# Hybrid attention and mLSTM block: the split halves of gate weights and mLSTM values put side by side, two products in place of three

## The reference

```
qk = silu(causal_depthwise_conv(concat(mq, mk)))
ig, fg = mi + i_bias, mf + f_bias              # two gates for each head and position
s   = (q @ k.T) * exp(D - m)                   # decays D from the gates, causal
num = s @ v ;  nq = sum(s)                     # over earlier positions
h   = num / max(|nq|, exp(-m))                 # then normalised over each head
```

## Time and profile before

| | |
|---|---|
| median of 3 runs | 349.46 us (348.89 to 349.79) |
| the profiled execution's own time | 346.94 us |
| its span in the trace | 345.2 us |
| PE busy | 325.0 us, 94% of the span |
| DVE busy | 208.4 us, 60% |
| ACT, POOL busy | 171.6 us (50%), 98.9 us (29%) |
| granted clock of TensorE, mean | 0.993 of full speed |

### The profile page before, as it was taken

One profiled execution on the slowest core, in us unless ns is written; L12 is line 12 of the kernel. 1 busy time (PEld: TensorE's weight loads), 2 busy tenths in 40 slices (PEclk: granted clock), 3 DMA queues, 4 the chain that ended last, 5 costly groups with the idle time before them and its releaser, 6 DMA issues.

```text
span 345.2 us, 5114 instructions
## 1 busy us (share of the span) xinstructions
PE 325.0 (94%) x1702; PEld 268.0 (78%) x1702; DVE 208.4 (60%) x499; ACT 171.6 (50%) x340; POOL 98.9 (29%) x121
## 2 busy tenths in 40 slices
PE   4999999999999999999999999899999999997790
PEld 3886688888888888888888887688888878886570
DVE  2534799667994599748964565455554632224646
ACT  4348553696263416834463513654557646445221
POOL 8001003208320240003400144860036624165250
PEclk9999999999999999999999999999999999999997
DMA  7831543853825542437333232100002400711133
GB/s 229 265 93 30 136 149 96 166 147 82 146 72 149 119 82 62 122 93 125 94 103 79 74 93 61 61 33 1 2 0 71 164 11 17 228 63 62 61 124 122
DMA packets 26346, 33.53 MB, mean 97 GB/s; under 512 B 3736, under 2 KB 14528, under 8 KB 26320
## 3 DMA queue, kind: packets, MB, share of 16 engines
q1 hardware_dynamic: 25184, 30.51, 29.8%
q0 software_dynamic: 1120, 2.68, 6.1%
q10 hardware_dynamic: 16, 0.00, 0.0%
HBM read 31.06 MB, written 2.13 MB: 96 GB/s over the span
## 4 chain that ended last, share of the span: by engine, by line
PE 86%; issue 4%; POOL 3%; DVE 3%; ACT 2%; DMA 1%; SPq 0%; DVEq 0%; POOLq 0%; ACTq 0%
PE bank L1312 24%; PE bank L1314 24%; PE bank L1313 24%; PE bank L1624 4%; PE bank L1594 3%; PE bank L1576 3%; DMA farena<-in_x 1%; POOL w_lo L582 1%; POOL farena L631 1%; PE bank L1333 1%; DVE farena L1253 1%; PE bank L1546 1%; PE bank L1480 1%; PE bank L1470 1%; DVE silu_az L1273 0%
## 5 line engine op out<-in xcount | busy, mean ns | idle before, releaser
L1312 PE MATMUL bank<-w_hi,xT_hi 128*128 128x512 f32 x288 | 117.5, 408 | 3.6 <-DVE farena L1253 2.2
L1314 PE MATMUL bank<-w_hi,xT_lo 128*128 128x512 f32 x288 | 113.2, 393 | 0.0
L1313 PE MATMUL bank<-w_lo,xT_hi 128*128 128x512 f32 x288 | 112.8, 392 | 0.0
L699 ACT ACTIVATE w_hi<-w_raw 128x512 fp32r<-128x512 f32 x88 | 53.1, 625 | 66.8 <-PE bank L1314 65.3
L1312 PEld LDWEIGHTS bank<-w_hi,xT_hi 128*128 128x128 f32 x288 | 54.7, 190 | 14.4 <-issue 3.8
L1314 PEld LDWEIGHTS bank<-w_hi,xT_lo 128*128 128x128 f32 x288 | 54.4, 189 | 12.0
L1313 PEld LDWEIGHTS bank<-w_lo,xT_hi 128*128 128x128 f32 x288 | 54.6, 190 | 9.5
L909 DVE TENSOR_TENSOR w_lo<-w_raw,w_hi 128x512 fp32r<-128x512 f32 x64 | 44.2, 699 | 15.4 <-ACT w_hi L699 15.0
L582 POOL TENSOR_TENSOR w_lo<-w_raw,w_hi 128x512 fp32r<-128x512 f32 x24 | 31.0, 1312 | 54.6 <-ACT w_hi L699 54.6
L1223 DVE TENSOR_TENSOR rarena<-bank,rarena 128x512 fp32r<-128x512 f32 (+3 forms) x32 | 15.6, 489 | 32.7 <-ACT rarena L851 32.7
L851 ACT ACTIVATE rarena<-bank 128x512 fp32r<-128x512 f32 (+3 forms) x32 | 13.8, 435 | 29.1 <-PE bank L1594 28.9
(11 more groups left out here) (175 smaller groups left out, 476.0 us busy)
## 6 DMA issues: line engine op xcount, KB each, us to landing
w_raw<-in_w_in SPq DMA_DIRECT2D x72, 256.0 KB, 2.8
w_raw<-in_w_out SPq DMA_DIRECT2D x16, 256.0 KB, 2.7
farena<-in_x SPq DMA_DIRECT2D x3, 512.0 KB, 8.4
farena<-g_rows POOLq DMA_DIRECT2D x4, 256.0 KB, 4.1
silu_az<-in_x SPq DMA_DIRECT2D x2, 512.0 KB, 4.5
w_raw<-in_x SPq DMA_DIRECT2D x2, 512.0 KB, 3.1
out_y<-silu_az SPq DMA_DIRECT2D x4, 256.0 KB, 2.1
out_y<-w_raw SPq DMA_DIRECT2D x4, 256.0 KB, 2.1
```

The costliest lines, as they stand in the source:

```text
L699: a.activation(w_hi[:, n % RING, :], w_raw[:, n % RAW, :], ACT.Copy).then_inc(w_hi_done, 1)
L1312: pe.matmul(o, hi, m_hi, start=start, stop=False)
L1313: pe.matmul(o, hi, m_lo, start=False, stop=False)
L1314: return pe.matmul(o, lo, m_hi, start=False, stop=stop)
```

## The change

The high and low gate weights go into one stationary `wg` of 128 columns: input high, forget high, input low and forget low, 16 columns at each multiple of 32, with zeros between. Each feature tile then takes two matmuls (by `xT_hi` and by `xT_lo`), which also adds the product of the low halves. A matrix `fold` (128 by 64, two identities of 64 on top of each other) sums the high and the low rows and replaces the slice of the identity. POOL clears `wg` and makes `fold`.

The halves of the mLSTM values lie side by side in `mv` (260 columns). For a position tile t and an earlier tile j, one matmul takes the high half of the scores by all 260 columns and one takes the low half by the first 130. The high and the low part of the result lie apart in `bank[7]`, and a new DVE step `head_sum` adds them into `num` in SBUF, where `head_stats` and `head_norm` read. Each position tile has a slot of its own, `ST_AT[h]` + 4 + t, and all use `bank[7]`, so PE waits before each one for the `head_sum` of the one before (`num_done`). The second half's `head_stats` and `head_norm`, the first half's too, come one loop number later. Some declarations of semaphores are left out below.

```diff
-PE_PV = {ST_AT[h] + NT + 2 * q: (h, q) for h in range(MH) for q in range(2)}
+PE_PV = {ST_AT[h] + NT + t: (h, t) for h in range(MH) for t in range(NT)}
...
-        wg_hi = sb("wg_hi", [P, NK, 32], F32R)
-        wg_lo = sb("wg_lo", [P, NK, 32], F32R)
+        wg = sb("wg", [P, NK, P], F32R)
+        fold = sb("fold", [P, P // 2])
...
+        num = sb("num", [P, 2, MV])
...
-        mv_hi = r_part(R_MV, NT, MH, MV)
-        mv_lo = r_part(R_MV + NT * MH * MV, NT, MH, MV)
+        mv = r_part(R_MV, NT * MH, 2 * MV)
-        gate_rows = gy[0:32, 1, 2, :]
+        gate_rows = gy[:, 1, 2, :]
...
+            g.memset(wg[:].bitcast(F32), 0.0).then_inc(wg_clear, 1)
...
+            g.wait_ge(ident_done, 1)
+            g.tensor_tensor(fold[:], ident[:, 0:P // 2], ident[:, P // 2:], ALU.add).then_inc(fold_done, 1)
...
-            g.memset(mv_hi[:, :, :, MD:MV].bitcast(F32), 1.0).then_inc(mv_ones, 1)
-            g.memset(mv_lo[:, :, :, MD:MV].bitcast(F32), 0.0).then_inc(mv_ones, 1)
+            g.memset(mv[:, :, MD:MV].bitcast(F32), 1.0).then_inc(mv_ones, 1)
+            g.memset(mv[:, :, MV + MD:].bitcast(F32), 0.0).then_inc(mv_ones, 1)
...
-                if b == S_MZ + 2:
+                if b == S_MZ + 3:
-                if b == S_MZ + 4:
+                if b == S_MZ + 5:
...
-                a.activation(mv_hi[:, t, :, 0:MD], bank[t][:].rearrange("p (h d) -> p h d", h=MH), ACT.Copy,
+                a.activation(mv[:, t * MH:(t + 1) * MH, 0:MD], bank[t][:].rearrange("p (h d) -> p h d", h=MH), ACT.Copy,
...
-            a.activation(rows[0], bank[7][0:16, :], ACT.Abs, bias=bcol[:, 1:2]).then_inc(absf_done, 1)
+            a.activation(rows[0], bank[7][32:48, :], ACT.Abs, bias=bcol[:, 1:2]).then_inc(absf_done, 1)
...
-                    a.wait_ge(mpv_ps, 2 * h)
+                    a.wait_ge(mpv_ps, NT * h)
...
-                v.scalar_tensor_tensor(out=mv_lo[:, t, :, 0:MD], in0=bank[t][:].rearrange("p (h d) -> p h d", h=MH),
-                                       scalar=rx[:, t:t + 1], in1=f32(mv_hi[:, t, :, 0:MD]), op0=ALU.mult,
+                v.scalar_tensor_tensor(out=mv[:, t * MH:(t + 1) * MH, MV:MV + MD], in0=bank[t][:].rearrange("p (h d) -> p h d", h=MH),
+                                       scalar=rx[:, t:t + 1], in1=f32(mv[:, t * MH:(t + 1) * MH, 0:MD]), op0=ALU.mult,
...
+            v.wait_ge(wg_clear, 1)
-                hi = wg_hi[:, :, 16 * q:16 * q + 16].rearrange("p k (j h) -> p k j h", j=NT)
-                lo = wg_lo[:, :, 16 * q:16 * q + 16].rearrange("p k (j h) -> p k j h", j=NT)
+                hi = wg[:, :, 32 * q:32 * q + 16].rearrange("p k (j h) -> p k j h", j=NT)
+                lo = wg[:, :, 64 + 32 * q:80 + 32 * q].rearrange("p k (j h) -> p k j h", j=NT)
...
-            v.tensor_tensor(gate_rows, bank[7][0:32, :], rbc[0:32, :], ALU.mult).then_inc(gate_sb, 1)
+            v.tensor_tensor(gate_rows, bank[7][:], rbc[:], ALU.mult).then_inc(gate_sb, 1)
...
             def gate_low():
-                v.tensor_scalar(rows[6], rows[6], bcol[:, 0:1], None, ALU.add).then_inc(igate_done, 1)
-                link(v.tensor_scalar(rows[3], bank[7][0:16, :], bcol[:, 1:2], 0.0, ALU.add, ALU.min))
+                v.tensor_scalar(rows[6], bank[7][0:16, :], bcol[:, 0:1], None, ALU.add).then_inc(igate_done, 1)
+                link(v.tensor_scalar(rows[3], bank[7][32:48, :], bcol[:, 1:2], 0.0, ALU.add, ALU.min))
...
+            def head_sum(h, t):
+
+                n = 2 * h + t // 2
+                v.wait_ge(mpv_ps, NT * h + t + 1)
+                if n:
+                    v.wait_ge(ym_done, n)
+                v.tensor_reduce(num[:, t % 2, :], bank[7][:, 0:2 * MV].rearrange("p (a c) -> p c a", a=2),
+                                mybir.AxisListType.X, ALU.add).then_inc(num_done, 1)
+
             def head_stats(n):
-                pv = bank[7 - n % 2][:, 0:2 * MV].rearrange("p (t c) -> p t c", t=2)
-                v.wait_ge(mpv_ps, n + 1)
+                pv = num
+                v.wait_ge(num_done, 2 * n + 2)
...
             def head_norm(n):
-                pv = bank[7 - n % 2][:, 0:2 * MV].rearrange("p (t c) -> p t c", t=2)
+                pv = num
...
-                if b - 3 in PE_PV:
-                    head_norm(2 * PE_PV[b - 3][0] + PE_PV[b - 3][1])
+                if b - 3 in PE_PV and PE_PV[b - 3][1] % 2 == 1:
+                    head_norm(2 * PE_PV[b - 3][0] + PE_PV[b - 3][1] // 2)
-                    head_stats(2 * PE_PV[b - 2][0] + PE_PV[b - 2][1])
+                    head_sum(*PE_PV[b - 2])
+                    if PE_PV[b - 2][1] % 2 == 1:
+                        head_stats(2 * PE_PV[b - 2][0] + PE_PV[b - 2][1] // 2)
...
-                    mm = product(bank[7][0:32, :], wg_hi[:, k, :], wg_lo[:, k, :], xT_hi[:, k, :], xT_lo[:, k, :],
-                                 k == 0, k == NK - 1)
+                    pe.matmul(bank[7][:], wg[:, k, :], xT_hi[:, k, :], start=k == 0, stop=False)
+                    mm = pe.matmul(bank[7][:], wg[:, k, :], xT_lo[:, k, :], start=False, stop=k == NK - 1)
...
-                if h and j == 0:
-                    pe.wait_ge(ym_done, 2 * h)
-            def head_values(h, half):
+            def head_values(h, t):
-                pe.wait_ge(pm_lo_done, NT * h + 2 * half + 2)
-                n = 2 * h + half
-                if n >= 2:
-                    pe.wait_ge(ym_done, n - 1)
-                for q in range(2):
-                    t = 2 * half + q
-                    for j in range(t + 1):
-                        w = slice(P_AT[j] + (t - j) * P, P_AT[j] + (t - j + 1) * P)
-                        mm = product(bank[7 - half][:, MV * q:MV * (q + 1)], pm_hi[:, w], pm_lo[:, w],
-                                     mv_hi[:, j, h, :], mv_lo[:, j, h, :], j == 0, j == t)
+                pe.wait_ge(pm_lo_done, NT * h + t + 1)
+                if h + t:
+                    pe.wait_ge(num_done, NT * h + t)
+                for j in range(t + 1):
+                    w = slice(P_AT[j] + (t - j) * P, P_AT[j] + (t - j + 1) * P)
+                    pe.matmul(bank[7][:, 0:2 * MV], pm_hi[:, w], mv[:, j * MH + h, :], start=j == 0, stop=False)
+                    mm = pe.matmul(bank[7][:, 0:MV], pm_lo[:, w], mv[:, j * MH + h, 0:MV], start=False, stop=j == t)
...
-            pe.matmul(bank[7][0:16, :], ident[0:32, 16:32], gate_rows, start=True, stop=True).then_inc(fgate_ps, 1)
+            pe.wait_ge(fold_done, 1)
+            pe.matmul(bank[7][0:P // 2, :], fold[:], gate_rows, start=True, stop=True).then_inc(fgate_ps, 1)
...
-                    pe.wait_ge(ym_done, 2 * MH)
+                    pe.wait_ge(num_done, MH * NT)

```

More of the change, by code:

```diff
@@ L313, in build @@
         wg_in = sem("wg_in")
+        wg_clear = sem("wg_clear")
+        fold_done = sem("fold_done")
         bias_in = sem("bias_in")
@@ L370, in build @@
         mpv_ps = sem("mpv_ps")
+        num_done = sem("num_done")
         var_done = sem("var_done")
```

## The result

The changed kernel takes 360.88 us (median of 4 runs, 360.72 to 360.99) against 349.17 us of the kernel before in the same runs: a ratio of 1.0333, 95% interval 1.0315 to 1.0351. That is slower by 11.7 us, and outside of the forecast range. The profiled execution took 360.72 us, its span is 358.6 us. TensorE's mean granted clock fell from 0.993 to 0.974.

What follows compares the result with a forecast made beforehand. PE, busy 94% of the span, was taken as the bound. Waits of 10.11 us less 4.32 (values) and 1.86 (gates) gave +3.93 on 349.46: slower, 353.4 us, range 350.3 to 356.6.

Steps and rivals of the forecast that it cites:

- the four places named: PE waits for head_sum at the second and fourth tile of head 0 and the fourth of heads 1 and 2.
- The third rival: PE's clock falls to 1.2 GHz in the new waits, some 1.2 us or more each: 355.8 to 358.2 us; chance 0.12.
- the product behind a wait of 0.88 us: Late in the kernel before, the product at 314.24 ran at the usual 0.47; taken as evidence against a clock fall.
- The waits: PE standing for head_sum: 2.70 and 1.68 us at head 0, 3.26 at head 1, 2.47 at head 2, together 10.11.
- The sum on DVE: Each of 16 added head_sum steps, 260 columns in: 0.43 us duration, 0.38 to the next instruction's start, bounds 0.3 and 0.68.
- The dear case of 0.68: Rival: each head_sum takes 0.68 us, adding 1.7 us over seven sums, 355.2 us; inside the forecast's own case of 0.70.
- PE's gain: Fewer PE matmuls save 1.86 us in the gates and 1.08 us a head, 4.32 for four, in the values.
- What was late next in `gate_rows`: The diagonal for rx_rows, ready at 34.25 against PE at 34.48, clears by 0.2 us, so the gates' gain holds.

Runs made afterwards that it cites:

- two_banks: The changed kernel with odd position tiles in bank 6, even ones in bank 7, so PE waits for the head_sum of two tiles back: 346.59 us, ratio 0.9946.
- before_again: The kernel before run once more, unchanged, for a second trace: 348.83 us against 349.26 in the other runs of the same kernel.
- thin_sum: The changed kernel with head_sum adding only the two denominator columns and leaving out the 128 values: 356.54 us, ratio 1.0212.
- two_banks_three: two_banks with the 260-column matmul split into two of 130, so three short products for a pair of tiles: 349.64 us, ratio 1.0001.
- gates_only: The kernel before with only the gate part of the change, values still in three products: 346.60 us, ratio 0.9939.

## Why the prediction was wrong

- **Direction and place: right.** Slower had 0.83, and the waits are at the four places named, none of weight at head 3. `two_banks` shows the cause by taking it away.
- **The clock: the step that failed.** The sum costed PE's work behind the waits at full speed, and so put the clock at nothing. The third rival had the mechanism (one fall behind each long wait) and even a price, 355.8 to 358.2, but a chance of 0.12 and no place in the sum. Three falls came, and each cost 1.66 to 1.68 us, not 1.2: at head 0 some eight products of 512 columns ran at the lower level, not five. That is 5.0 of the error of 7.5. I let one row speak against it, the product behind a wait of 0.88 us, taken from one execution. `before_again` shows the same product in another execution, with the fall. Nor is it so that no wait of before is as long as those forecast: from 324.75 us on PE waits 1.81 us for `farena`, longer than the 1.68 forecast at head 0's fourth tile, and the clock stays up behind it. The Trainium skill, TensorE: Matmul & The Clock Gate, section What's actually happening, warned that the throttled state is the default and comes back with idleness, and that the point of the change differs from run to run. The traces agree with both: three falls here, and a start that differs by 0.98 us with one code.
- **The waits: 11.14 us lost, 10.11 forecast.** For the three long ones 2.83, 3.89 and 3.46 against 2.70, 3.26 and 2.47. On DVE the distance from the start of a head's second sum to the end of its third was 8.12 us at head 0 and 8.89 at head 1, against 7.57 and 8.36 in my sum. `head_norm` was mis-sized: 0.89, not 0.60. Its two halves take 0.34 each from SBUF (0.60 for both, as they overlap), not 0.28, and I had costed it as in a pipeline, where the next step starts before the last one ends, but `head_sum` behind it waits for `ym_done`, so it pays up to the end. For the same reason a sum costs 0.46 up to the statistics that wait for it, not 0.38. The convolution took 3.97, not 3.80. At head 2 its first steps have POOL's inverse root and masks beside them, which I had moved without a price; that they slow DVE is argued from the times, not shown. Head 0's fourth tile went the other way, 0.76 for 1.68: the clock had held PE 1.7 us back, so DVE had time to catch up. The two errors hid each other there.
- **The sum on DVE: right.** 0.42 to 0.43 us in all 16, as taken. The dear case of 0.68 didn't come. `thin_sum` shows that the price mattered little: with 0.27 us less for each sum the long waits are 0.3 to 0.9 us shorter, of 2.7 to 3.7.
- **PE's gain: 3.63 of 4.32 in the values, 1.80 of 1.86 in the gates.** The pair's pitch was near enough (0.233 for 0.228 from one tile of head 1 to the next), but two more tiles on their own in each head bring two more changes between shapes, of some 0.05 us each. `two_banks_three` confirms that the pair beats the triple. By the formula of the Trainium skill, TensorE: Matmul & The Clock Gate, section Back-to-back issue gap, triple and pair would cost about the same; the timelines disagree, 0.32 against 0.22 us.
- **What was late next in `gate_rows`: right.** `rx_rows` was not held up: 1.80 of the 1.86 us came. That POOL's clear cost nothing fits, but wasn't tested alone: `gates_only` starts 0.4 us later than the kernel before in one trace, `before_again` without any clear 0.98.
- **Not in the sum:** 0.2 us at head 0's scores, where PE, now early, waits for the weighted scores. `gates_only` has them too.

Put together: +3.93 forecast. Clock +5.0, waits +1.0, values' gain +0.7, gates' gain +0.1 and scores +0.2 make +10.9, the measured shift between like starts. The medians differ by 11.7; the last 0.8 I put down to the clock at the start and the end, in which executions of one kernel differ by up to 2.6 us (`before_again` against the first trace), but that is argued.

## What to carry to other kernels

Price a new wait on TensorE as its length plus a fall of the clock that may come behind it (here 1.7 us each), unless the engine has other work on its queue, and don't excuse it by one execution that shows none. When a result buffer is reused at once, follow the consumer's engine in order through everything that stands before the read; a second buffer took away 10 us of waits here that a cheaper consumer didn't. When a wait goes, look at what was hidden behind it: two further steps of DVE came up and ate nearly the whole gain of the values. Moving them forward took 1.7 us off the median, but only 0.8 in the heads of the trace, and only one of the two waits went.

## What the runs showed of the hardware that was not expected

- The length of a wait of PE alone doesn't decide if the clock falls. It fell behind waits of 2.67, 3.73 and 3.30 us (the kernel after), 1.73 and 2.43 (`thin_sum`), 0.88 (`before_again`) and 1.34 (late in `gates_only`), and not behind 2.41 and 3.19 (`thin_sum`), 2.0 (`two_banks`), 0.88, 1.81 and 1.34 (the first trace of the kernel before). What else decides is open. Behind the wait of 1.73 the fall came 0.9 to 1.0 us after PE had begun to work again. In the mLSTM each fall of the kernel after cost 1.66 to 1.68 us, at the level of 1.2 GHz, with a pitch of 0.43 us in place of 0.23 for 512 columns.
- Around 130 to 260 columns a matmul with a new stationary hardly gets dearer: some 0.11 us for 130 and 0.12 for 260 (a pair's 0.23 less 0.11), against 0.23 for 512. The second 130 columns were nearly free, the next 250 were not.
- A wait of PE can make the next one shorter through its own slow clock (head 0: 0.76 instead of 1.68 us), so that two costs don't add.
